# The last four units of a stage and the first four of the next by halves of the tokens, and setup's sum shared by two engines

## The reference

```python
for i in range(2):
    mod = silu(c) @ ada_w[i] + ada_b[i]
    sh1, sc1, g1, sh2, sc2, g2 = jnp.split(mod, 6, axis=-1)
    h = modulate(rms_norm(x, norm_g[i, 0]), sh1, sc1)
    y = nsa_mixer(h, ...) if i == 0 else swa_sink_mixer(h, ...)
    x = x + (1 + g1) * rms_norm(y, norm_g[i, 1])
    h = modulate(rms_norm(x, norm_g[i, 2]), sh2, sc2)
    y = squared_relu_mlp(h, w_up, w_down)
    x = x + (1 + g2) * rms_norm(y, norm_g[i, 3])
x = x + hybrid_mixer(rms_norm(x, norm_mix))
x = x + memory_cross_attention(rms_norm(x, norm_xattn), rms_norm(mem, norm_mem))
x = x + conv_ffn(rms_norm(x, norm_ffn))
out = rms_norm(x, norm_final)
```

## Time and profile before

| | |
|---|---|
| median of 3 runs | 2273.28 us (2271.47 to 2274.64) |
| the profiled execution | 2274.38 us, its span 2272.6 us |
| busy: PE, DVE, POOL, ACT | 2050.0 (90%), 1140.3 (50%), 906.0 (40%), 692.8 (30%) |
| chain that ended last | issue 44%, PE 27%, POOL 19%, DVE 4%, DMA 3%, ACT 1% |
| read from HBM | 235.21 MB, 110 GB/s over the span |
| one unit: load from issue to landing, ACT's rounding, POOL's rest | 3.5 (median), 1.05, 2.47 |
| mean granted clock of PE | 0.937 of full speed |

### The profile page before, as it was taken

The page is one execution under the profiler, slowest core; times in us unless marked ns, Lnnn a source line. Parts: engine busy times, 40 slices in busy tenths (PEclk is TensorE's granted clock), DMA queues, the critical chain, the costliest instruction groups (busy, mean ns, idle before and its releaser), DMA issues.

```text
span 2272.6 us, 26962 instructions
## 1 busy us (share of the span) xinstructions
PE 2050.0 (90%) x10312; PEld 1667.5 (73%) x10312; DVE 1140.3 (50%) x1673; ACT 692.8 (30%) x1199; POOL 906.0 (40%) x513
## 2 busy tenths in 40 slices
PE   7988999799999979797999998895889698999997
PEld 6868777588888857675888886684768366888886
DVE  5575776675564555536352443374332325626354
ACT  2333563322222232533222223223223223222222
POOL 1455554244444424642444443230236023444442
PEclk9998999799999979897999999895899698999999
DMA  6645333345555314411323232220134012333331
GB/s 260 194 182 178 107 89 121 102 172 180 188 183 185 122 55 156 144 52 47 102 93 102 93 97 89 61 74 23 38 121 130 28 48 73 102 93 93 100 94 65
DMA packets 78664, 252.16 MB, mean 111 GB/s; under 512 B 10840, under 2 KB 11352, under 8 KB 78296
## 3 DMA queue, kind: packets, MB, share of 16 engines
q1 hardware_dynamic: 78552, 250.61, 33.7%
HBM read 235.21 MB, written 15.37 MB: 110 GB/s over the span
## 4 chain that ended last, share of the span: by engine, by line
issue 44%; PE 27%; POOL 19%; DVE 4%; DMA 3%; ACT 1%; SPq 1%; POOLq 0%; DVEq 0%; ACTq 0%
POOL wl L736 17%; PE ps L796 6%; PE ps L797 6%; PE ps L798 6%; PE ps L1008 2%; PE ps L951 2%; PE ps L980 1%; DMA qscr<-rot_ls 1%; DMA qscr<-rot_l 1%; PE ps L1241 1%; POOL pr L757 1%; DMA raw<-in_units 1%; ACT pr L2100 1%; PE ps L1218 1%; SPq L583 1%
## 5 line engine op out<-in xcount | busy, mean ns | idle before, releaser
L736 POOL TENSOR_TENSOR wl<-raw,wh 128x1024 fp32r<-128x1024 f32 x309 | 761.7, 2468 | 1246.8 <-ACT wh L1977 1246.8
L1977 ACT CAST wh<-raw 128x1024 fp32r<-128x1024 f32 x309 | 323.7, 1050 | 1139.7 <-PE ps L798 1045.5
L796 PE MATMUL ps<-ah,wh 128*128 128x512 f32 x1512 | 601.7, 398 | 26.7 <-DVE al L1333 13.7
L797 PE MATMUL ps<-ah,wl 128*128 128x512 f32 x1512 | 593.8, 393 | 0.0
L798 PE MATMUL ps<-al,wh 128*128 128x512 f32 x1512 | 593.8, 393 | 0.0
L796 PEld LDWEIGHTS ps<-ah,wh 128*128 128x128 f32 x1512 | 286.5, 190 | 104.5 <-issue 25.2
L798 PEld LDWEIGHTS ps<-al,wh 128*128 128x128 f32 x1512 | 287.0, 190 | 60.6
L797 PEld LDWEIGHTS ps<-ah,wl 128*128 128x128 f32 x1512 | 287.7, 190 | 57.3 <-issue 0.7
L796 PE MATMUL ps<-hh,wh 128*128 128x512 f32 x688 | 268.5, 390 | 3.9 <-DVE hl L1934 3.9
L798 PE MATMUL ps<-hl,wh 128*128 128x512 f32 x688 | 267.7, 389 | 0.0
L797 PE MATMUL ps<-hh,wl 128*128 128x512 f32 x688 | 267.7, 389 | 0.0
(11 more groups left out here) (287 smaller groups left out, 2401.9 us busy)
## 6 DMA issues: line engine op xcount, KB each, us to landing
raw<-in_units SPq DMA_DIRECT2D x309, 512.0 KB, 3.5
ada_mlp<-in_ada SPq DMA_DIRECT2D x64, 512.0 KB, 3.5
ada<-in_ada SPq DMA_DIRECT2D x16, 512.0 KB, 15.7
qs<-qscr SPq DMA_DIRECT2D x32, 256.0 KB, 3.5
ada_in<-in_ada SPq DMA_DIRECT2D x16, 512.0 KB, 3.7
ks<-kscr SPq DMA_DIRECT2D x24, 256.0 KB, 4.9
x<-in_xT SPq DMA_DIRECT2D x1, 2048.0 KB, 13.8
qscr<-rot_h SPq DMA_DIRECT2D x8, 256.0 KB
```

Source lines behind the costliest of these rows:

```text
L736: nc.gpsimd.tensor_tensor(wl[:, slot], raw[:, slot], wh[:, slot].bitcast(F32), ALU.subtract).then_inc(lo_done, 1)
L796: nc.tensor.matmul(out_ap, wh[:, slot, k], high[:, k0 + k], start=first and k == 0, stop=False)
L797: nc.tensor.matmul(out_ap, wl[:, slot, k], high[:, k0 + k], start=False, stop=False)
L1977: a.copy(wh[:, slot], raw[:, slot]).then_inc(hi_done, 1)
```

## The change

PE (`gemm_tail`): the first four units of a tail are multiplied as before. The last four are multiplied for tokens 0 to 255 one after the other, then for tokens 256 to 511, with matmuls 256 wide. The sums of squares of the first half, its spread, and at double joints the sums of the new x's squares stand between the units of the second half. `gemm_head` does the same with the first four units of the next stage: first half of all four, then second half, with the second half's sums and spreads between them. DVE and ACT do `double`, `single` or the output by halves: every addition, multiplication and norm that was 512 tokens wide is now two, of 256; the inversions are on 64 rows in place of 128. The x squares go into the tile y (`x_squares`). `wait`s on `half_done` and `half_read` tie PE and DVE at the halves. SP waits for the chunks of both halves before its load of the rotary tables (t_made of 40, where it was 24). ACT's load of the root's table is moved from the eighth unit of the tail to the fourth, and its rounding of the eighth unit ahead (`highs(u + RING + 7)`) stands behind the root of x's first half. The final norm and its DMAs go by halves too.

Setup: PE sums the scale over chunks 8 to 11 only; DVE sums chunks 12 to 15 into `acc1`, which PE adds with eight matmuls; the loads are reordered for that; DVE's first inversion is now behind this sum and ahead of the shift's last four steps.

The diff, cut to its core (single on ACT and the other call sites follow the same pattern):

```diff
@@ setup's DMAs @@
-        for n in (2, 10, 3, 4, 11, 5, 12):
+        for n in (10, 2, 11, 3, 12, 13, 14, 15):
             sp.dma_start(ada0[:, n], src["ada"][n]).then_inc(ada_in[n], 16)
         units(0, 1)
-        for n in (6, 7, 13):
+        for n in (4, 5, 6, 7):
             sp.dma_start(ada0[:, n], src["ada"][n]).then_inc(ada_in[n], 16)
-        units(1, 2)
-        for n in (14, 15):
-            sp.dma_start(ada0[:, n], src["ada"][n]).then_inc(ada_in[n], 16)
-        units(2, RING)
+        units(1, RING)
@@ tensor @@
+        def half_spread(bank, slot, h):
+            roots[0] += 1
+            pe.wait_ge(inv_made, roots[0])
+            for j in (2 * h, 2 * h + 1):
+                mm = nc.tensor.matmul(ps[:, bank, j * P:(j + 1) * P],
+                                      small("quarter")[ROWS[h], j:j + 1].to_broadcast([64, P]), rs[ROWS[h], slot, 0:P],
+                                      start=True, stop=True)
+            mm.then_inc(spread, 1)
+        def out_sums(h):
+            pe.wait_ge(sq_added, added[0] + (6, 9)[h])
+            quarters(4 + h, sqs[:, HALF[h]], True, False, S // 2, 2 * h)
+            pe.wait_ge(sq_made, made[0] + (8, 12)[h])
+            quarters(4 + h, sq[:, 1, HALF[h]], False, True, S // 2, 2 * h).then_inc(sq_used, 1)
+            if h:
+                added[0] += 9
+                made[0] += 12
+        def x_sums(h, first, last):
+            for c in range(first, last):
+                pe.wait_ge(xsq_made, xmade[0] + c + 1)
+                mm = quarters(6 + h, y[:, c, HALF[h]], c == 0, c == DC - 1, S // 2, 2 * h)
+                mm.then_inc(sq_used, 1)
+            if last == DC:
+                xmade[0] += DC
+        def gemm_tail(first, high, low, double, ready=None, ks=DC, midway=None):
+            gemm(first, 4, high, low, ready=ready, ks=ks)
+            n0 = done[0]
+            for h in range(2):
+                for i in range(4):
+                    u = first + 4 + i
+                    if h == 0:
+                        bank_free(n0 + i)
+                        pe.wait_ge(lo_done, u + 1)
+                    else:
+                        pe.wait_ge(half_read, halves[0] + i + 1)
+                    mm = products(ps[:, (n0 + i) % RING, HALF[h]], u % RING, high[:, :, HALF[h]], low[:, :, HALF[h]], ks=ks)
+                    mm.then_inc(unit_used if h else half_done, 1)
+                    if h == 0 and i == 2 and midway:
+                        midway()
+                    if h == 1 and i == 0:
+                        out_sums(0)
+                    elif h == 1 and i == 1:
+                        half_spread(4, 0 if double else 1, 0)
+                    elif h == 1 and i == 2 and double:
+                        x_sums(0, 0, 3)
+            done[0] += 4
+            halves[0] += 4
+            if double:
+                x_sums(0, 3, 6)
+                out_sums(1)
+                x_sums(0, 6, DC)
+                half_spread(5, 0, 1)
+                half_spread(6, 1, 0)
+        def gemm_head(first, high, low, ready, double):
+            n0 = done[0]
+            for h in range(2):
+                for i in range(4):
+                    u = first + i
+                    if h == 0:
+                        bank_free(n0 + i)
+                        pe.wait_ge(lo_done, u + 1)
+                    mm = products(ps[:, (n0 + i) % RING, HALF[h]], u % RING, high[:, :, HALF[h]], low[:, :, HALF[h]],
+                                  ready=(a_ready, ready + DC * h))
+                    if h:
+                        mm.then_inc(unit_used, 1)
+                    elif double and i == 1:
+                        x_sums(1, 0, 5)
+                    elif double and i == 2:
+                        x_sums(1, 5, DC)
+                    elif double and i == 3:
+                        half_spread(7, 1, 1)
+                    elif not double and i == 0:
+                        out_sums(1)
+                    elif not double and i == 1:
+                        half_spread(5, 1, 1)
+            done[0] += 4
...
         square_sums()
-        for k in range(2, 6):
+        for k in range(2, 4):
             scale_part(k)
-        root_spread(1)
-        for k in range(6, 8):
-            scale_part(k)
+        root_spread()
+        pe.wait_ge(scale_part_made, 4)
+        for m in range(8):
+            mm = nc.tensor.matmul(ps[:, 7, m:m + 1], acc1[:, m * P:(m + 1) * P], small("ones")[:, 0:1],
+                                  start=False, stop=m == 7)
+        mm.then_inc(scale_sum, 1)
...
-        gemm_squared(FIRST["nsa_out"], ah, al, 0, ready=(o_split, 0), midway=lambda: ada_late(0))
-        square_sums()
+        gemm_tail(FIRST["nsa_out"], ah, al, True, ready=(o_split, 0), midway=lambda: ada_late(0))
         mlp("mlp0", 0)
-        square_sums()
-        gemm(FIRST["swa_in"], UNITS_SWA_IN, ah, al, ready=(a_ready, A_READY["swa_in"]))
+        gemm_head(FIRST["swa_in"], ah, al, A_READY["swa_in"], True)
+        gemm(FIRST["swa_in"] + 4, UNITS_SWA_IN - 4, ah, al)
@@ vector @@
+        def tail_out(one, beside, meanwhile=None):
+            def add(at, a, b, cols, count):
+                dve.wait_ge(sq_made, made[0] + count)
+                if at:
+                    dve.wait_ge(sq_added, added[0] + at)
+                v.tensor_tensor(sqs[:, cols], a, b, ALU.add).then_inc(sq_added, 1)
+            every = slice(0, S)
+            for c in range(4):
+                one(c, bank(), every).then_inc(evac, 1)
+                if meanwhile:
+                    meanwhile(c)
+                if c == 2:
+                    add(0, sq[:, 0], sq[:, 1], every, 2)
+                elif c == 3:
+                    add(1, sq[:, 0], sqs, every, 3)
+            for i in range(4):
+                dve.wait_ge(half_done, halves[0] + i + 1)
+                one(4 + i, ps[:, (banks[0] + i) % RING], HALF[0]).then_inc(half_read, 1)
+                if i == 0:
+                    add(2, sq[:, 1], sqs, every, 4)
+                else:
+                    add(2 + i, sq[:, (3 + i) % 2, HALF[0]], sqs[:, HALF[0]], HALF[0], 4 + i)
+            for i in range(4):
+                one(4 + i, bank(), HALF[1]).then_inc(evac, 1)
+                if i:
+                    add(5 + i, sq[:, (3 + i) % 2, HALF[1]], sqs[:, HALF[1]], HALF[1], 8 + i)
+                if i < 3:
+                    beside(i)
+            made[0] += 12
+            added[0] += 9
+            halves[0] += 4
+        def double(one, layer, which, gain, shift, meanwhile=None, between=None):
+            inv = []
+            def beside(i):
+                if i == 0:
+                    rms(0, ROWS[0])
+                    if between:
+                        between()
+                elif i == 1:
+                    inv.append(spread_of(4, HALF[0]))
+                    add_y(layer, which, 0, inv[0], 0, 3)
+                else:
+                    add_y(layer, which, 0, inv[0], 3, 6)
+            tail_out(one, beside, meanwhile)
+            add_y(layer, which, 0, inv[0], 6, DC)
+            rms(0, ROWS[1])
+            rms(1, ROWS[0])
+            inv_y = spread_of(5, HALF[1])
+            dve.wait_ge(x_new, x_news[0])
+            norm(x, gain, shift, ah, al, HALF[0], spread_of(6, HALF[0]))
+            add_y(layer, which, 1, inv_y, 0, DC)
+            rms(1, ROWS[1])
+            dve.wait_ge(x_new, x_news[0])
+            norm(x, gain, shift, ah, al, HALF[1], spread_of(7, HALF[1]))
+        def single(gain):
+            inv = []
+            def one(c, b, cols):
+                return v.tensor_tensor(x[:, c, cols], b[:, cols], x[:, c, cols], ALU.add)
+            def beside(i):
+                if i == 0:
+                    rms(1, ROWS[0])
+                elif i == 1:
+                    inv.append(spread_of(4, HALF[0]))
+                    norm(x, gain, None, ah, al, HALF[0], inv[0], first=0, last=3)
+                else:
+                    norm(x, gain, None, ah, al, HALF[0], inv[0], first=3, last=6)
+            tail_out(one, beside)
+            norm(x, gain, None, ah, al, HALF[0], inv[0], first=6, last=DC)
+            rms(1, ROWS[1])
+            norm(x, gain, None, ah, al, HALF[1], spread_of(5, HALF[1]))
...
             dve.wait_ge(ada_first, k + 1)
-        rms(1)
+            if k != 3:
+                continue
+            for i in range(4):
+                dve.wait_ge(ada_in[12 + i], 16)
...
+                op.then_inc(scale_part_made, 1)
+                dve.wait_ge(scale_part_made, i + 1)
+            rms(1)
@@ scalar @@
+        def tail(u, out_t, n, beside):
+            def square(c, cols, wait, added_to):
+                act.wait_ge(wait[0], wait[1])
+                act.wait_ge(*((sq_added, added[0] + added_to) if added_to else (sq_used, used[0])))
+                a.activation(sq[:, c % 2, cols], out_t[:, c, cols], ACT.Square).then_inc(sq_made, 1)
+            for c in range(4):
+                highs(u + RING + c, u + RING + c + 1)
+                if c == 3:
```

(46 more changed lines are left out.)

390 lines of the change are left out of this document (195 added, 195 removed).

## The result

| | median, us | ratio to before |
|---|---|---|
| before | 2274.64 (2269.85 to 2278.48, 19 runs) | |
| changed | 2277.75 (2275.05 to 2281.91, 19 runs) | 1.0017 (95%: 1.0011 to 1.0024) |

The forecast was 2261, faster by 0.5%; the change makes the kernel slower by 0.17%, outside the range. Spans of the profiled executions: 2272.6 and 2273.9. The forecast was a difference of -12.3 between such executions and it is +1.3, so 13.6 us are missing. (The medians differ by more, 3.1: the changed kernel's profiled execution, 2275.65, lies 2.1 under its median.)

What follows compares the result with a forecast made beforehand. PE, busy nine tenths, loses 138.3 us at six joints to a chain through DVE. Joints -14.3, mlp0 +8.0, mlp1 +2.5, setup -6.5, end -2.0 give -12.3: 2261.0 us in the median, range 2248 to 2272.

Steps and rivals of the forecast that it cites:

- Setup -6.5: Start of the kernel: first product at 46.3 in place of 52.76, DVE being the later engine; -6.5 us (-8.6 to -3).
- The end -2.0: After PE's last product: the last chain has half the evacuation, sums and chunks, less the cost of halves; -2.0 us.
- mlp0 +8.0: MLP behind the joint: DVE sets the block's end, PE waits 7.2 for `hl` and loses 0.8 to the clock; +8.0 us.
- mlp1: Same wait on DVE in the second MLP, which has no adaLN steps and catches up; +2.5 us (0 to 4).
- Double joints: Four joints with y and x norms, cut in halves: 26.3 us typically, 27.3 before mlp0, 25.3 before mix_in; together 105.2.
- the 2.7: Double joint: PE's wait ahead of its last half unit for x squares' sums, with one DVE block by POOL; 2.7 us.
- the 8.8: Double joint: from the tail's end to the head's first product, with one block by POOL; 8.8 us.
- Single joints: Two joints without a y norm, the first half normed beside the tail: 9.4 us each, 18.8 together.
- The 4.6 for the first half unit: Single joint: the head's first unit runs at the norm's pace; 4.6 us of the 9.4.
- edits at nothing: SP's later wait before the rotary tables and swa_in's unit 4, and ACT's eighth rounding: hidden, put at 0 us.
- The one on the other side of zero: Slower rival: PE stays at 1.2 GHz in the head, 6.8 us per double joint, 27 for four; 2288, chance 0.08.
- The third: Rival: joints bring nothing, locks twice or longer x sums, about +5 in the MLPs, setup and end remain; 2270, chance 0.12.

Runs made afterwards that it cites:

- e2: Changed kernel with the joints ahead of mlp0 and of swa_in 512 wide as before; 2264.62 us, ratio to before 0.9961.
- e5: Changed kernel with halves only at the joint ahead of ffn and at the end, the five other joints 512 wide; 2266.12 us, ratio to before 0.9969.
- e6: Changed kernel with all six joints 512 wide, setup and end as changed; 2268.12 us, ratio to before 0.9977.
- e9: Changed kernel, complete, with the scaled chunk in PSUM for double joints' additions to x and single joints' norms; 2259.79 us, ratio to before 0.9942.
- e1: Changed kernel with only the joint ahead of swa_in 512 wide as before; 2272.3 us, ratio to before 0.9993.
- e3: Changed kernel with only units 0 and 1 of swa_in's head by halves, units 2 and 3 whole behind them; 2273.66 us, ratio to before 0.9998.
- e7: Changed kernel with POOL's low parts of the three units beside each tail's second half cut to 8 columns; 2258.6 us, ratio to before 0.9933.
- e4: Changed kernel with seven adaLN steps of mlp0's first up block cut to 8 of 1024 columns; 2271.68 us, ratio to before 0.9992.
- e10: e9 with the joints ahead of mlp0 and swa_in 512 wide as before; 2254.4 us, ratio to before 0.9913.
- e8: e6 with each VectorE operation of add_y and norm issued as two of 256 tokens; 2289.41 us, ratio to before 1.0077.

## Why the prediction was wrong

The sum had six terms. Against the profiled execution (-12.3 forecast, +1.3 measured):

- **Setup -6.5: right, -6.1.** PE after:

```profile
24.67 6.99 PE L1142 MATMUL ps<-cond,ada 128*128 128x1 f32 x32
31.75 2.08 PE L878 MATMUL ps<-rs,sm 128*128 128x128 f32 x8
33.62 3.41 PE L1154 MATMUL ps<-sm,acc 128*128 128x1 f32 x16
39.20 3.58 PE L982 MATMUL ps<-sm,acc 128*128 128x1 f32 x16 [2.17 <-DVE acc L1597]
46.68 0.76 PE L807 MATMUL ps<-ah,wh 128*128 128x512 f32 x1 [3.90 <-DVE al L1426]
```

  The first product starts at 46.68 (46.3 forecast), with DVE the later one at `acc0` as said.
- **The end -2.0: right** from unit 308 on (from +3.3 to +1.3, and 2.0 in e2, e5 and e6 too).
- **mlp0 +8.0: right in kind, 9.6.** The waits for `hl` are the 7.4 of the list, for 7.2 forecast. The granted clock behind them is what was put too low: it stood at 0.50 from 491.2 to 501.4, for 13 products 0.43 apart where 0.23 is usual, so about 2.6 and not 0.8. The loss is larger than the 2.9 that the joint had gained; e2 shows it. mlp1: +1.3 for 2.5.
- **Double joints: 105.2 forecast, 112.6 less 3.7 for the adaLN sums = 108.9.** They are 3.7 dearer, and no single step carries that. In the joint ahead of mlp1 (27.9 where 26.3 were forecast) PE's timeline gives 2.6 for the half-width products (2.4 forecast), 1.6 for y's sums and spread (1.0), 2.4 for the wait ahead of the last half unit (2.7), 8.5 up to the head's first product (8.8), 3.6 and 3.7 for the two first half units (3.0 each), 2.4 for the waits and sums of the second half (2.2), 2.6 for its spread (2.4) and 0.5 for the clock (0.8). Most is missing at the norm's pace, in the rows the last product of the tail and the first and last of the head's first half unit:

```profile
1038.84 0.28 PE L809 MATMUL ps<-al,wh 128*128 128x256 f32 x1
...
1047.45 0.55 PE L807 MATMUL ps<-ah,wh 128*128 128x256 f32 x1 [1.94 <-DVE al L1426]
...
1053.80 0.41 PE L809 MATMUL ps<-al,wh 128*128 128x256 f32 x1
```

  The locks were in the forecast, one in the 2.7 and one in the 8.8, and are there: 2.0 and 1.8, one in each group of additions. Without them (e9) the four joints cost 5.1 less.
- **Single joints: 9.4 each forecast, 12.5 and 11.2 measured.** Here the prediction had no lock at all. "The first half is normed beside the tail" is the sentence that fails. This norm has two SBUF inputs in each low part, and POOL's two low parts stand just there. In the joint ahead of xq the head's second half unit, put at no more than 0.4 for the clock, costs 2.2 and the sums and spreads 3.1 for 2.0. The 4.6 for the first half unit came out (4.5), but by luck: it was put down to the norm's pace, and without locks (e9) it is 0.7. The two blocked low parts:

```profile
1648.43 2.02 DVE L1424 TENSOR_TENSOR al<-tt,ah 128x256 fp32r<-128x256 f32 x1
...
1651.74 2.41 DVE L1424 TENSOR_TENSOR al<-tt,ah 128x256 fp32r<-128x256 f32 x1
```

- **The step that is missing: swa_in, +6.1.** For mlp0 I asked what DVE has to do behind the joint, and for swa_in not; "edits at nothing" names only SP's load there. DVE's end of the norm was 5.5 later and the rotary chain passed it on to the end of attention (e1, e3). This step was put at nothing without a reason, and with the 8.6 that the joints fell short (3.7 double, 4.9 single) it makes 14.7. The rest is small and of both signs: mlp0 and mlp1 together +0.4, setup +0.4, the clock in ffn (below) +1.6, and gains that were not forecast, 2.7 in nsa and 0.7 elsewhere. Together 13.7, against 13.6 missing.

Of the rivals none came true as put. The one on the other side of zero named the clock. By the stretch of the joint ahead of mlp1 the granted clock rose instead, from 0.76 to 0.88; the sign came from DVE. The third came nearest, but it had only about 5 given back. The rival that was missing is my own mlp0 term in a second place: a stage that is bound by DVE behind each of the first two joints.

The Trainium skill has a rule that I passed over: "VectorE: DVE Perf Modes", section "The TRN2 errata — SBUF-src ops pay a fixed extra latency per instruction", says that VectorE's operations with SBUF sources are slower than specified by a fixed cost per instruction, and not by a factor. The trace agrees in kind: 475 ns for half of what takes 743. I had used the half-width rows for the pace of the norm, but never counted them over the joint (some 40 more operations, 7 us of DVE). The lock's other side is in the Trainium skill, "SBUF — State Buffer", section "Who interferes with whom": a VectorE instruction with at most one SBUF input, outside the modes that use two ports, doesn't contend with GpSimd. e9 agrees: 716 ns fell to 476 with the first input in PSUM.

## What to carry to other kernels

Cutting a dependent chain in halves hides one half behind other work, but it lengthens the chain itself: each operation had a fixed part here, and the inversion, halved in its rows, didn't shrink at all. So ask for both ends: when the engine at the joint can restart, and when the engine that carries the chain is done, and then which of the two the next stage hangs on. Where new overlap sets a VectorE operation beside GpSimd, give it one of its inputs from PSUM; here this was worth 14.4 us.

## What the runs showed of the hardware that wasn't expected

- The inversion of 64 rows takes as long as that of 128 (0.95 both, with 128 columns).
- Where several engines pass a chunk along, a lock cost the chain more than its own length: 6.0 and 4.7 us per single joint for some 3.5 of blocked operations (e7). A part of that is PE's granted clock, 0.92 in the stretch ahead of xq and 1.00 without the locks (e9).
- Half-width products next to each other stand 0.120 apart at full clock in the joints, as the 0.1195 of the earlier trace rows; each group of short sums or spreads between them has 0.2 ahead of it and 0.2 behind, and one product behind it comes 0.22 after the last.
- In the ffn of the changed kernel PE's granted clock falls to 0.5 for 3.4 us from 2231.97 on, behind a wait for `hl` of 2.2 that stands there before too, and 1.6 us are lost to it by unit 308. It is so in e1, e4, e7, e9 and e10, and not before nor in e2, e3, e5, e6 and e8, though the instructions are the same there in e2, e3, e5 and the changed kernel. What decides it stays open.
